# HGRN block: the sample states' product moved ahead of the recurrence, and matmuls on constants after each distance

## The reference

```
G = cumsum(log_f);  Gl = G[last]
o_inter = (q * exp(G)) @ S                            # reads of the state
A[i, j] = sum_k q[i,k] * k[j,k] * exp(G[i,k] - G[j,k])   for j <= i
o = o_inter + A @ v
S = S * exp(Gl) + (k * exp(Gl - G)).T @ v             # the new state
```

## Time and profile before

| | us |
|---|---|
| median of 3 runs | 2412.63 (2411.06 to 2412.84) |
| profiled execution, its own time | 2412.28 |
| its span | 2410.5 |
| hgrn block, first layer, from 175.5 to 245.3 of the span | 69.8 |
| TensorE busy in the span | 2287.9 |
| VectorE busy in the span | 1522.2 |
| mean granted TensorE clock | 0.959 |

### The profile page before, as it was taken

How to read it: one execution, slowest core, us unless ns; L and a number is a source line. 1 busy time by engine, 2 the same in 40 slices (tenths; PEclk the granted TensorE clock), 3 DMA queues, 4 the chain that set the end, 5 groups by cost and what they waited for, 6 DMA issues and landing times. The chain is left out here.

```text
span 2410.5 us, 58546 instructions
## 1 busy us (share of the span) xinstructions
PE 2287.9 (95%) x20514; PEld 2092.8 (87%) x20514; DVE 1522.2 (63%) x3131; ACT 1232.7 (51%) x2351; POOL 1095.7 (45%) x1000
## 2 busy tenths in 40 slices
PE   6978989999999999999989789999999999999998
PEld 4944868999998799999979357799999987999997
DVE  2747644973225968888656566379532268787885
ACT  3530224558556955555536202155675578555554
POOL 0005104884445746566300231078744466565661
PEclk8978899999999999999989689999999999999999
DMA  6475024555553079889544740345555511898992
GB/s 268 161 266 207 3 103 153 183 183 192 191 188 109 0 256 313 284 305 313 175 151 158 270 159 12 132 166 180 188 199 189 186 53 70 282 313 276 313 308 103
DMA packets 123821, 455.53 MB, mean 189 GB/s; under 512 B 13744, under 2 KB 14256, under 8 KB 122544
## 3 DMA queue, kind: packets, MB, share of 16 engines
q1 hardware_dynamic: 105264, 386.80, 44.4%
q0 software_dynamic: 18432, 67.12, 9.9%
HBM read 449.37 MB, written 4.49 MB: 188 GB/s over the span
## 5 line engine op out<-in xcount | busy, mean ns | idle before, releaser
L415 POOL TENSOR_TENSOR parts<-ring,parts 128x512 fp32r<-128x512 f32 x358 | 464.1, 1299 | 471.2 <-ACT parts L408 456.2
L408 ACT ACTIVATE parts<-ring 128x512 fp32r<-128x512 f32 x616 | 386.8, 632 | 358.7 <-PE ps_u L464 281.5
L460 PE MATMUL ps_u<-h_parts,parts 128*128 128x256 f32 x4096 | 563.2, 280 | 0.9 <-ACT parts L408 0.6
L2584 PE MATMUL ps_y<-act_parts,parts 128*128 128x256 f32 x4096 | 562.8, 279 | 0.0
L460 PEld LDWEIGHTS ps_u<-h_parts,parts 128*128 128x128 f32 x4096 | 514.9, 188 | 3.2 <-ACT parts L408 1.9
L2584 PEld LDWEIGHTS ps_y<-act_parts,parts 128*128 128x128 f32 x4096 | 514.2, 188 | 0.9 <-ACT parts L2524 0.3
L415 DVE TENSOR_TENSOR parts<-ring,parts 128x512 fp32r<-128x512 f32 x258 | 177.4, 691 | 381.3 <-ACT parts L408 358.7
L2633 POOL TENSOR_TENSOR act_parts<-big,act_parts 128x256 fp32r<-128x256 f32 x256 | 247.0, 965 | 304.1 <-ACT act_parts L2613 304.1
L464 PE MATMUL ps_u<-h_parts,parts 128*128 128x256 f32 x2048 | 322.2, 279 | 0.9 <-DVE parts L415 0.6
L2588 PE MATMUL ps_y<-act_parts,parts 128*128 128x256 f32 x2048 | 322.3, 279 | 0.0
L464 PEld LDWEIGHTS ps_u<-h_parts,parts 128*128 128x128 f32 x2048 | 275.7, 188 | 1.5 <-DVE parts L415 0.8
(11 more groups left out here) (391 smaller groups left out, 2890.1 us busy)
## 6 DMA issues: line engine op xcount, KB each, us to landing
ring<-in_stream SPq DMA_DIRECT2D x522, 512.0 KB
more_ring<-in_stream SPq DMA_DIRECT2D x126, 512.0 KB
extra_ring<-in_stream SPq DMA_DIRECT2D x48, 512.0 KB, 5.4
big<-in_stream SPq DMA_DIRECT2D x16, 512.0 KB, 11.6
out_state_out<-big SPq DMA_DIRECT2D x2, 1440.0 KB, 9.1
big<-in_state SPq DMA_DIRECT2D x2, 1280.0 KB, 10.8
big<-in_mixc SPq DMA_DIRECT2D x2, 1024.0 KB, 8.1
big<-in_spots SPq DMA_DIRECT2D x2, 1024.0 KB, 5.4
```

Source lines behind the costliest of these rows:

```text
L408: eng.activation(m.parts[:, q % PARTS, 0, :], half_tile(m, t, half), ACT.Copy).then_inc(s["hi_ready"], 1)
L415: eng.tensor_tensor(m.parts[:, q % PARTS, 1, :], half_tile(m, t, half), m.parts[:, q % PARTS, 0, :].bitcast(F32), ALU.subtract).then_inc(m ...
L460: pe.matmul(out, hi[:, k, :], hr[:, side, kk, 0:tokens], start=(kk + side == 0), stop=False)
L2584: pe.matmul(ps[:, half * KD // 2 + k, :], hi[:, k, :], act_parts[:, j % AHEAD, side, :], start=False, stop=False)
```

## The change

The sample states' product is made inside the loop over distances, after distance 4, from values that GpSimd now makes first and that lie in `after` (a tensor the recurrence fills later), into banks 2 and 3 of `ps_outer`. VectorE makes the sample states before the last `values`. Where step 1 reuses those banks, TensorE waits for a new semaphore, `sample_out`. GpSimd's turns and the counts of `vm_ready` and `u_ready` move by one. After each of the distances 2 to 7 four matmuls of `keep_busy` are issued, into bank 2 of `ps_sums`.

```diff
--- before.py
+++ after.py
@@ -976,7 +976,7 @@
     TB = P // C
     TOK = ((0, P), (P, P), (NP, NB * NS))
     names = ("step pool_step lb_ready lb_out f_ready gates_ready qt_ready pairs_ready sums_ready kt_ready turned "
-             "kt_out values_done vm_ready u_ready u_out scan_ready inter_ready products_ready rows_out cols_ready "
+             "kt_out values_done vm_ready u_ready u_out sample_out scan_ready inter_ready products_ready rows_out cols_ready "
              "cols_out")
     with signals(nc, names) as s, nc.psum_tensor("ps_sums", [P, 3, 512], F32) as ps_sums, \
             nc.psum_tensor("ps_outer", [P, 4, 512], F32) as ps_outer, nc.Block() as block:
@@ -1003,6 +1003,9 @@
         ada_rows = m.zact[:, 8, 0:2 * P]
         o = m.mixed[:, 0:2, :]

+        def sample_values(h):
+            return after[0:NB * NS, 1, h * NB:(h + 1) * NB, :]
+
         def blocks(x, sample, lo, hi):

             x, c = (x[:, :, NP:NT], NS) if sample else (x[:, :, 0:NP], C)
@@ -1078,21 +1081,21 @@

             def mask_v(turn):

-                if turn < 4:
-                    tt, hb, n = turn // 2, turn % 2, P
-                    mask = m.mix("block_rows")[:, hb * TB // 2:(hb + 1) * TB // 2]
-                else:
-                    tt, n, mask = 2, NB * NS, m.mix("batch_rows")[0:NB * NS, :]
+                tt, hb = turn // 2, turn % 2
+                mask = m.mix("block_rows")[:, hb * TB // 2:(hb + 1) * TB // 2]
                 if turn >= 2:
-                    pool.wait_ge(s["u_ready"], 2 * turn - 2)
+                    pool.wait_ge(s["u_ready"], 2 * turn - 1)
                 for h in range(4):
-                    i = pool.tensor_tensor(vm[0:n, turn % 2, h, :, :],
-                                         spread(vtok[0:n, tt, h * HD:(h + 1) * HD], 1, TB // 2),
-                                         spread(mask[0:n], 2, HD), ALU.mult)
+                    i = pool.tensor_tensor(vm[:, turn % 2, h, :, :], spread(vtok[:, tt, h * HD:(h + 1) * HD], 1, TB // 2),
+                                           spread(mask, 2, HD), ALU.mult)
                 i.then_inc(s["vm_ready"], 1)

             pool.wait_ge(s["kt_out"], 3)
-            for turn in range(5):
+            for h in range(4):
+                i = pool.tensor_tensor(sample_values(h), spread(vtok[0:NB * NS, 2, h * HD:(h + 1) * HD], 1, NB),
+                                       spread(m.mix("batch_rows")[0:NB * NS, :], 2, HD), ALU.mult)
+            i.then_inc(s["vm_ready"], 1)
+            for turn in range(4):
                 mask_v(turn)

         @block.tensor
@@ -1131,9 +1134,18 @@
                 mm.then_inc(s["turned"], 1)
             for d in range(2, C):
                 distance(d)
+                keep_busy(pe, m, ps_sums[:, 2, :], 4)
                 if d == 5:
                     turn(2)
                 ada(*((26, 28), (28, 30), (30, 32), (32, 33), (33, 35), (35, 37))[d - 2])
+                if d == 4:
+                    pe.wait_ge(s["vm_ready"], 1)
+                    for pair in range(A_PAIRS):
+                        for r in range(2):
+                            rows = slice(r * HD, (r + 1) * HD)
+                            mm = pe.matmul(ps_outer[rows, 2 + pair, :], ktt[0:NB * NS, 2, pair, rows],
+                                           sample_values(2 * pair + r), start=True, stop=True)
+                    mm.then_inc(s["u_ready"], 1)
             def inter(pair, r, t, n, state):

                 rows = slice(r * HD, (r + 1) * HD)
@@ -1151,9 +1163,11 @@

             for step in range(4):
                 tt = step // 2
-                pe.wait_ge(s["vm_ready"], step + 1)
+                pe.wait_ge(s["vm_ready"], step + 2)
                 for pair in range(A_PAIRS):
                     n = 2 * step + pair
+                    if n == 2:
+                        pe.wait_ge(s["sample_out"], 1)
                     if n >= 4:
                         pe.wait_ge(s["u_out"], n - 3)
                     for r in range(2):
@@ -1177,14 +1191,6 @@
                     ada(38 + 2 * step, 40 + 2 * step)
             ada(46, 48)
             read_states(2)
-            pe.wait_ge(s["vm_ready"], 5)
-            pe.wait_ge(s["u_out"], 8)
-            for pair in range(A_PAIRS):
-                for r in range(2):
-                    rows = slice(r * HD, (r + 1) * HD)
-                    mm = pe.matmul(ps_outer[rows, pair, :], ktt[0:NB * NS, 2, pair, rows], vm[0:NB * NS, 0, 2 * pair + r, :, :],
-                                   start=True, stop=True)
-            mm.then_inc(s["u_ready"], 1)
             mm = read_states(3)
             mm.then_inc(s["inter_ready"], 1)
             turn(4)
@@ -1246,10 +1252,17 @@
             for d in range(2, C):
                 pairs(d)
                 values(d - 1)
+            ve.wait_ge(s["u_ready"], 1)
+            for pair in range(A_PAIRS):
+                new = m.states[:, pair, 1:, :]
+                last = blocks(since, True, NS - 1, NS)[:, pair, :, :].broadcast_to([P, NB, HD])
+                link(ve.tensor_tensor(new, m.state0[:, pair, :, :], last, ALU.mult))
+                link(ve.tensor_tensor(new, new, ps_outer[:, 2 + pair, :].rearrange("p (b v) -> p b v", b=NB), ALU.add))
+            ve.sem_inc(s["sample_out"], 1)
             values(C - 1)
             ve.sem_inc(s["values_done"], 1)
             for turn in range(4):
-                ve.wait_ge(s["u_ready"], 2 * turn + 2)
+                ve.wait_ge(s["u_ready"], 2 * turn + 3)
                 for j in range(TB // 2):
                     b = turn * TB // 2 + j
                     for pair in range(A_PAIRS):
@@ -1262,12 +1275,6 @@
                         link(i)
                 ve.sem_inc(s["scan_ready"], 1)
                 ve.sem_inc(s["u_out"], 2)
-            ve.wait_ge(s["u_ready"], 9)
-            for pair in range(A_PAIRS):
-                new = m.states[:, pair, 1:, :]
-                last = blocks(since, True, NS - 1, NS)[:, pair, :, :].broadcast_to([P, NB, HD])
-                link(ve.tensor_tensor(new, m.state0[:, pair, :, :], last, ALU.mult))
-                link(ve.tensor_tensor(new, new, ps_outer[:, pair, :].rearrange("p (b v) -> p b v", b=NB), ALU.add))
             ve.wait_ge(s["inter_ready"], 1)
             link(ve.tensor_tensor(o[:, :, C:], o[:, :, C:], ps_sums[:, 0:A_PAIRS, C:NT], ALU.add))

```

## The result

The forecast is wrong. The changed kernel takes 2427.82 us (median of ten runs, 2421.31 to 2432.88) against 2412.74 before on the same chip (ten runs, 2410.21 to 2418.75); the ratio is 1.0062, interval 1.005 to 1.0075. 2407 was forecast. The profiled execution takes 2426.41, its span 2424.6.

The account below looks back on a forecast made before the run. In the HGRN block, VectorE's recurrence was taken as bounding, then TensorE's tail of sample product and state reads. Per layer -3.26 + 0.5 and -3.15 + 0.5, together -5.4 us, gave 2407 us; range 2403 to 2412.

Parts of the forecast that it names:

- The tail: After the recurrence, the sample product leaves TensorE's path: 3.26 and 3.15 us gained, reads still 3.16 us at the lower clock.
- rival A: The tail's state reads also run at the higher clock, another 1.37 us per layer; 2404.3 us, chance 0.17.
- The constants: Matmul groups between distances hold the clock at 1.00; 0.9 us per group, TensorE's 8.27 us of work shrinking to 4.7.
- The start of the recurrence: TensorE's added work ahead of step 0 delays the recurrence by 0.5 us per layer, bounds -0.5 and +2.
- about one of the seven per GpSimd instruction: Between distances, VectorE ends one two-SBUF-input instruction per 1.04 us GpSimd instruction; distance 6's products ready at about 210.0.
- The cover of 0.9 us: Ahead of the recurrence, 0.9 us of VectorE's idle time is left; slowdown by GpSimd beyond it would lengthen the path.
- The rule of the Trainium skill: Ports shared by GpSimd and VectorE lock for a whole instruction; worst case one GpSimd instruction's length per VectorE instruction.
- My own bound: The forecast is wrong as a whole if the recurrence starts over 3 us later than before.
- Rival C: Groups between distances don't hold the clock; step 0 9.9 us later, +6.7 us per layer, 2425.7 us, chance 0.07.
- Rival B: Clock falls again between distances, or GpSimd slows VectorE more: 1.5 to 2 us per layer, 2410 to 2411, chance 0.2.
- Rival D: No effect: in the tail the reads wait for something else that ended with the product; 2412 us, chance 0.03.

Follow-up runs that it names:

- mask_128: Changed kernel with the four sample masks over 128 rows instead of 32, read from the second tile's tokens (wrong sample states); 2407.16 us, ratio 0.9975.
- break_timed: Changed kernel plus one wait of GpSimd on its own four 32-row sample masks before the 128-row masks, timed over ten runs; 2405.77 us, ratio 0.9968.
- break_no_busy: As break_timed, but without the constant matmuls; 2412.3 us, ratio 0.9992.
- wide: Changed kernel with the sample masks over 128 rows and right values, GpSimd clearing the sample tokens' tile at the block's start; 2410.4 us, ratio 0.9992.
- wide_no_busy: As wide, but without the constant matmuls; 2410.62 us, ratio 1.0.
- busy_only: Kernel before the change with only the constant matmuls added after distances 2 to 7, product not moved; 2418.93 us, ratio 1.0023.
- move_only: Changed kernel without the 24 constant matmuls per layer, product still moved; 2423.42 us, ratio 1.0039.
- turn0_first: Changed kernel with the four masks of turn 0 put ahead of the 32-row sample masks on GpSimd; 2411.16 us, ratio 0.9985.
- one_wide: As wide, but only the first sample mask has 128 rows and the other three 32; one run, 2403.67 us.
- one_wide_timed: The kernel of one_wide, timed in rounds; 2418.15 us, ratio 1.0022.
- one_narrow: As wide, but the first sample mask has 32 rows and the other three 128; one run, 2406.93 us.
- mask_late: Changed kernel with GpSimd's 32-row sample masks made after turn 1 and the sample product after distance 7; 2420.83 us, ratio 1.0034.
- narrow_break: Changed kernel with GpSimd waiting for its own four 32-row sample masks before turn 0; one run, 2405.38 us.
- narrow_cleared: As wide, with GpSimd's clearing, but all four sample masks over 32 rows; one run, 2423.61 us.

## Why the prediction was wrong, point by point

**The tail: right, and too small.** The product left it, and the reads L1152 start 0.11 us behind the recurrence's end (250.04). From the recurrence's last instruction to the next block's VectorE, 8.6 us became 4.1, so 4.5 per layer instead of 3.2. The mis-sized term is the reads: 2.05 us, not 3.16, because the clock falls at 251.5, near their end, and not ahead of them. That was rival A, which had 1.37 us per layer for what came as 3.16 - 2.05 = 1.11. It isn't steady: in mask_128 the reads take 1.80 us in layer one and 3.16 in layer two, and the tails 3.6 and 5.2.

**The constants: right in their size and in what they hold, where nothing stalls; not in what that is worth.** A group takes 1.03 us at the higher level against 0.9 forecast. With them the clock is 1.00 from 194.00 to 214.40 in mask_128 and in the stretch of break_timed, and 0.50 in that of break_no_busy. But they shorten the way from the values of distance 2 to the recurrence by at most 0.3 us a layer (17.04 or 17.05 us in break_timed and wide, 17.09 to 17.36 in break_no_busy and wide_no_busy). The medians say 6.5 us in break_timed, 0.2 in wide and a loss of 6 in busy_only; most of that isn't in the block, and isn't explained. After the stall, at the lower level, they cost 23.46 - 18.30 = 5.2 us in layer one; in layer two, where the level was back sooner, the changed kernel needs 17.73 us and move_only 19.21.

**The start of the recurrence: this is the step that failed.** Its term was +0.5 us a layer, at most +2, and it measured +13.8 and +8.5. What was wrong in it is the sentence that GpSimd slows VectorE by "about one of the seven per GpSimd instruction", so that four more masks cost four VectorE instructions one mask's length each. I had put a mask of 32 rows down as a mask like the others, since it takes the same 1.04 us. It isn't: at the head of GpSimd's run such masks held one VectorE instruction for 8.98 us, some eight masks long. Without the stall the step holds: mask_128 starts its recurrence 39.7 and 40.4 us into the block, before 40.4 and 40.6, forecast + 0.5. The cover of 0.9 us on VectorE didn't matter, since the delay came ahead of TensorE's work and took the clock with it. The rule of the Trainium skill (SBUF — State Buffer, section "Who interferes with whom"), a lock for a whole instruction, by which I set the worst case, doesn't reach as far as the 8.98 us row, in which eight instructions went by. My own bound that the forecast is wrong as a whole if the recurrence starts over 3 us later was passed in both layers.

**Rival C** had 2425.7 for a time close to the measured one, with the groups not holding the clock. Its clock was seen (0.52 and 0.50), and its price of constants at the lower level with it; its cause wasn't: the same groups hold the clock in mask_128. Rival B named the slowdown by GpSimd and gave it 1.5 to 2 us. Rival D is out, since the tails moved.

**What the runs show of the cause, and what they don't.** The stall comes in every layer in which the first VectorE instruction with two SBUF inputs meets GpSimd's run in a 32-row mask that has another one behind it, and behind that 128-row masks with no wait between. It stays away when the run begins with 128-row masks and VectorE comes in one of these (mask_128, wide, wide_no_busy, turn0_first, one_wide, layer two of one_wide_timed), when only the first mask has 32 rows (one_narrow), when the run begins with turn 0 and GpSimd pauses for step 0 behind the 32-row ones (mask_late), and when GpSimd waits before the 128-row ones (narrow_break, break_timed, break_no_busy). That this height and this unbroken run decide is shown, by pairs that differ in nothing else (wide against narrow_cleared, the changed kernel against narrow_break), in every one of the 15 layers with the condition and in none of the others. Why it is so, no run shows. Nor was a run made with two 32-row masks, or with 32-row ones alone and nothing behind them, so how many it takes isn't known. Open too is why the clock falls more often outside the block in some kernels.

## What to carry to other kernels

Where two engines work on SBUF at once, read the price of contention from rows of the same pair of shapes, not from equal durations: here two masks of the same 1.04 us held VectorE very differently. After such a move look first for a single instruction far above its usual time; here it was one row of 8.98 us against 1.27. And before a gain is given up, part the mechanisms: one wait on GpSimd's own work turned a loss of 15 us into a gain of 6, and the single run of one_wide would have misled, since a stall there turned on 0.7 us of alignment. When matmuls on constants raise the clock, check what the stretch waits for: here the way to the recurrence took 17.05 us at 1.00 and 17.28 at a mean of 0.70.

## What was not expected of the hardware

- A run of GpSimd tensor_tensor of 32x512 and then 128x512 blocked one VectorE tensor_tensor with both inputs in SBUF for 8.1 to 9.4 us, while one with an operand in PSUM went by beside the first mask (L1238, 0.56 us from 195.20).
- GpSimd's 32x512 takes as long as its 128x512: while VectorE is blocked both start 1.01 us apart (195.22 to 199.27 for four, 199.27 to 204.32 for five). Beside VectorE, in mask_128, the 128x512 takes 1.15 (4.60 / 4).
- TensorE's idle time of 8.52 and 8.29 us brought the clock from 1.00 to 0.50 in both layers, but it came back at very different times: 3.3 us after the work began again in layer two (at 1408.6, from 1405.26), and 15.9 us after it in layer one (at 224.2, from 208.28), though TensorE was busy there for 5.20 of the first 5.20 us.
